# Fixed sets of PSUM banks for the MLP panels, layer norm features a tile sooner, and gates with 16 stationary columns

## The reference

```python
def sqrelu_mlp(x, w_up, w_down):
    return jnp.square(jax.nn.relu(x @ w_up)) @ w_down

for layer in range(2):
    if layer == 0:
        mix = ... @ w_out_even
    else:
        h = x @ w_in_odd                 # 1024 x 3088: q, k, v, and fl, one gate for each of 16 heads
        qf, kf, vf, fl = _split(h, ODD_SPLITS)
        mix = forgetting_attention(qf, kf, vf, fl, fox_f_bias) @ w_out_odd
    x = layer_norm(ALPHA * x + mix, gain[layer, 0], bias[layer, 0])
    x = layer_norm(ALPHA * x + sqrelu_mlp(x, w_up, w_down), gain[layer, 1], bias[layer, 1])
```

## Time and profile before

| | |
|---|---|
| median of three executions | 2456.62 us |
| profiled execution, its own time | 2456.84 us |
| its span in the profile | 2455.5 us |
| mean TensorE clock granted, of full speed | 0.959 |
| PE busy | 2286.5 us, 93% |
| DVE busy | 1043.5 us, 42% |
| ACT busy | 703.8 us, 29% |

### The profile page before, as it was taken

The page is one execution under the profiler, slowest core; times in us unless marked ns, Lnnn a source line. Parts: engine busy times, 40 slices in busy tenths (PEclk is TensorE's granted clock), DMA queues, the critical chain, the costliest instruction groups (busy, mean ns, idle before and its releaser), DMA issues.

```text
span 2455.5 us, 28478 instructions
## 1 busy us (share of the span) xinstructions
PE 2286.5 (93%) x11871; PEld 1686.7 (69%) x11871; DVE 1043.5 (42%) x1904; ACT 703.8 (29%) x1188; POOL 95.4 (4%) x96
## 2 busy tenths in 40 slices
PE   7998899979989999899788989999999999899998
PEld 6866687864434343587555778888787777788887
DVE  5347465342322233434566534233521455342335
ACT  4324354310100010223345223133223362231331
POOL 2001001010000000000000000000000000000000
PEclk9989899989999999999889999999989999999999
DMA  5232242359999999522100222323132201223230
GB/s 194 86 127 82 78 163 105 102 223 392 427 426 427 426 428 427 203 81 69 69 1 1 90 100 103 103 86 103 36 132 86 86 2 39 100 102 103 86 103 34
DMA packets 106740, 370.34 MB, mean 151 GB/s; under 512 B 15040, under 2 KB 20672, under 8 KB 94320
## 3 DMA queue, kind: packets, MB, share of 16 engines
q1 hardware_dynamic: 103584, 361.65, 39.1%
q0 software_dynamic: 3024, 6.83, 0.9%
HBM read 368.38 MB, written 4.19 MB: 152 GB/s over the span
## 4 chain that ended last, share of the span: by engine, by line
PE 78%; DMA 10%; DVE 8%; ACT 2%; issue 1%; POOL 1%; SPq 0%; DVEq 0%; ACTq 0%; POOLq 0%
PE PB L450 52%; PE PB L1898 8%; PE PB L467 5%; PE PB L460 4%; PE PB L769 4%; DMA Z<-in_w_exp_gate 4%; PE PB L661 3%; DMA FL_raw<-in_w_exp_gate 1%; DMA FH_raw<-in_w_exp_gate 1%; DMA Z<-in_w_exp_down 1%; PE PB L785 1%; DVE W L442 1%; DMA FL_raw<-in_w_exp_down 1%; PE PB L666 1%; ACT W L434 1%
## 5 line engine op out<-in xcount | busy, mean ns | idle before, releaser
L442 DVE TENSOR_TENSOR W<-R,W 128x2048 fp32r<-128x2048 f32 (+1 forms) x128 | 291.4, 2277 | 663.1 <-ACT W L434 663.0
L450 PE MATMUL PB<-W,FH 128*128 128x512 f32 (+1 forms) x1792 | 558.4, 394 | 8.1 <-DVE FL L823 6.7
L434 ACT ACTIVATE W<-R 128x2048 fp32r<-128x2048 f32 (+1 forms) x128 | 243.5, 1903 | 678.8 <-PE PB L450 671.7
L450 PEld LDWEIGHTS PB<-W,FH 128*128 128x128 f32 x1792 | 332.4, 190 | 77.4 <-DVE FL L823 8.1
L450 PE MATMUL PB<-W,hid 128*128 128x512 f32 x1536 | 349.6, 389 | 1.0 <-DVE X L2923 1.0
L450 PE MATMUL PB<-W,FL 128*128 128x512 f32 (+1 forms) x896 | 348.8, 389 | 0.0
L450 PE MATMUL PB<-FH,W 128*128 128x512 f32 (+1 forms) x1152 | 327.4, 369 | 15.6 <-ACT nsp L2878 14.3
L450 PEld LDWEIGHTS PB<-W,hid 128*128 128x128 f32 x1536 | 288.1, 188 | 61.0 <-DVE X L2923 1.4
L450 PEld LDWEIGHTS PB<-FH,W 128*128 128x128 f32 x1152 | 210.7, 191 | 52.1 <-ACT nsp L2878 14.7
L450 PE MATMUL PB<-FL,W 128*128 128x512 f32 (+1 forms) x576 | 212.2, 368 | 0.0
L450 PEld LDWEIGHTS PB<-W,FL 128*128 128x128 f32 x896 | 169.7, 189 | 35.4
(11 more groups left out here) (329 smaller groups left out, 2643.8 us busy)
## 6 DMA issues: line engine op xcount, KB each, us to landing
R<-in_mlp_w_up SPq DMA_DIRECT2D x32, 1024.0 KB, 5.3
R<-in_mlp_w_down SPq DMA_DIRECT2D x32, 1024.0 KB, 5.0
Z<-in_w_exp_down SPq DMA_DIRECT2D x14, 2048.0 KB, 30.6
Z<-in_w_exp_up SPq DMA_DIRECT2D x13, 2048.0 KB, 36.4
R<-in_w_exp_gate SPq DMA_DIRECT2D x11, 2048.0 KB, 32.3
W_raw<-in_w_exp_up SPq DMA_DIRECT2D x10, 2048.0 KB, 31.3
R<-in_w_exp_up SPq DMA_DIRECT2D x9, 2048.0 KB, 30.9
R<-in_w_in SPq DMA_DIRECT2D x12, 1024.0 KB, 5.4
```

The source lines that it names most:

```text
L434: k.A.e.activation(w.splits[w.split_of[u]][0][:, 0:m], w.rows(u), ACT.Copy).then_inc(*w.hi.tick(u))
L442: k.V.e.tensor_tensor(wl[:, 0:m], w.rows(u), wh[:, 0:m].bitcast(F32), ALU.subtract).then_inc(*w.lo.tick(u))
L450: ins = te.matmul(bank, l, r, start=(start and n == 0), stop=(stop and n == len(terms) - 1), skip_group_check=True)
```

## The change

**Banks.** The first up panel still takes four banks of PANELS. These four are now set 0 of the layer, and the other four banks are set 1. Up panel j takes set j mod 2, and down half h takes set h. The last down half of layer 0 takes the two banks of set 1 that are not in FLIPS, and the first two of set 0. In both layers set 0 comes out as banks 4, 5, 0, 1 and set 1 as 2, 3, 6, 7.

**Features.** DVE makes the low part of tile 0's features after centring tile 1 (before: tile 2), and that of tile 1 after centring tile 2 (before: behind tile 2's scale and a cut of weights). ACT makes the high parts of both ahead of a cut that stood between them. PE turns tile 0 one step of 12 products earlier.

**Gates.** ACT and DVE cut the 16 gate columns into `forget_hi` and `forget_lo` (128 x 128 each). PE takes them as the stationary operand, 16 columns wide, and moves the 512 tokens of FH and FL: 24 products into the first 16 partitions of a bank. DVE copies that out (16 x 512), PE turns it in four turns behind the second step of the next panel, into a bank of FLIPS, and the logarithms go on from there.

```diff
+    def numbers(self, keys):
+        return tuple(self.banks.index(self.where[key]) for key in keys)
...
+        self.forget_w = [nc.alloc_sbuf_tensor_at(name, [P, KT, 16], FR, offset=self.z_at + 4 * at)
+                         for name, at in (("forget_hi", 16128), ("forget_lo", 16256))]
... act_out_ln
     act_features(k, ("ln", n), 0)
+    act_features(k, ("ln", n), 1)
     act_cut(k, u0 + 4)
-    act_features(k, ("ln", n), 1)
... dve_out_ln, and with other units dve_mlp
         dve_ln_center(k, n, i)
-        if i == 2:
-            dve_features(k, ("ln", n), 0)
+        if i in (1, 2):
+            dve_features(k, ("ln", n), i - 1)
         if i == 3:
             dve_cut(k, u0 + 5)
         dve_ln_scale(k, n, i)
         if i == 2:
             dve_cut(k, u0 + 4)
-            dve_features(k, ("ln", n), 1)
... pe_ln_behind
-    return {5: lambda: pe_ln(k, n, 0), 6: lambda: pe_ln(k, n, 1)}
+    return {4: lambda: pe_ln(k, n, 0), 6: lambda: pe_ln(k, n, 1)}
... pe_mlp
-            banks = [k.banks.take(T, ("up", layer, c, j, f), k.relued.at(layer, c, j, f),
-                                  of=Banks.PANELS if first else Banks.ALL) for f in range(4)]
+            keys = [("up", layer, c, j, f) for f in range(4)]
+            banks = [k.banks.take(T, key, k.relued.at(*key[1:]), of=Banks.PANELS if first else fours[j % 2]) for key in keys]
+            if first:
+                fours = [k.banks.numbers(keys)]
+                fours.append(tuple(b for b in Banks.ALL if b not in fours[0]))
...
-            of = Banks.PANELS if (c, half) == (1, 1) else Banks.ALL
+            of = fours[half]
+            if (c, half) == (1, 1) and layer == 0:
+                of = tuple(b for b in fours[1] if b not in Banks.FLIPS) + fours[0][0:2]
...
-                if (layer, c, half) == (0, 1, 1) and (q, i) in ((3, 2), (2, 3)):
+                if (layer, c, half) == (0, 1, 1) and (q, i) in ((2, 2), (2, 3)):
                     pe_ln(k, 1, i - 2)
... pe_odd
+    def turn_gates():
+        bank = k.banks.take(T, ("flog",), k.dve_step.at("forget", "logits"), of=Banks.FLIPS)
+        T.wait_ge(*k.dve_step.at("forget", "copied"))
+        flips(k, bank, [k.o_gates[:, 128 * i:128 * i + 128] for i in range(NT)]).then_inc(*k.pe_step.tick("forget"))
...
-                   behind=({} if p else {1: lambda: pe_ln(k, 1, 2), 2: lambda: pe_ln(k, 1, 3)}))
+                   behind={0: {1: lambda: pe_ln(k, 1, 2), 2: lambda: pe_ln(k, 1, 3)}, 1: {1: turn_gates}}.get(p, {}))
         if p == 0:
-            bank = k.banks.take(T, ("flog",), k.dve_step.at("forget", "logits"))
-            T.wait_ge(*k.c6_in.at(3))
-            for i in range(NT):
-                at = slice(128 * i, 128 * i + 128)
-                ins = group(te, bank[:, 16 * i:16 * i + 16],
-                            [(F[:, c, at].bitcast(F32), k.o_wf[:, c, :]) for F in (k.FH, k.FL) for c in range(KT)])
-            ins.then_inc(*k.pe_step.tick("forget"))
+            bank = k.banks.take(T, ("gates",), k.dve_step.at("forget", "copied"))
+            T.wait_ge(*k.dve_step.at("forget", "parts"))
+            terms, (wh, wl) = [], k.forget_w
+            for c in range(KT):
+                terms += three((wh[:, c, :], wl[:, c, :]), (k.FH[:, c, :], k.FL[:, c, :]))
+            products(te, bank[0:16, :], terms, True, True).then_inc(*k.pe_step.tick("gates by head"))
... act_odd, first panel
+            A.wait_ge(*k.c6_in.at(3))
+            ae.activation(k.forget_w[0][:], k.o_wf, ACT.Copy).then_inc(*k.act_step.tick("forget", "high"))
... dve_odd, first panel
+            V.wait_ge(*k.act_step.at("forget", "high"))
+            ve.tensor_tensor(k.forget_w[1][:], k.o_wf, k.forget_w[0][:].bitcast(F32), ALU.subtract).then_inc(
+                *k.dve_step.tick("forget", "parts"))
... dve_forget
+    V.wait_ge(*k.pe_step.at("gates by head"))
+    ve.tensor_copy(k.o_gates, k.banks["gates",][0:16, :]).then_inc(*k.dve_step.tick("forget", "copied"))
```

More of the change, by code:

```diff
@@ L2883, in act_mlp @@
         for n in range(8):
-            if layer == 0 and c and n >= 6:
-                act_features(k, ("ln", 1), n - 6)
+            if layer == 0 and c and n == 6:
+                act_features(k, ("ln", 1), 0)
+                act_features(k, ("ln", 1), 1)
             if u0 + 10 + n < end:
@@ L2929, in dve_mlp @@
                 if (c, half) == (1, 1):
-                    if layer == 0 and i == 2:
-                        dve_features(k, ("ln", 1), 0)
+                    if layer == 0 and i in (1, 2):
+                        dve_features(k, ("ln", 1), i - 1)
                     if layer == 0 and i == 3:
@@ L2936, in dve_mlp @@
                         dve_cut(k, u0 + 16)
-                        dve_features(k, ("ln", 1), 1)
             if (c, half) != (1, 1):
@@ L2961, in odd_views @@
     k.o_lf, k.o_fb = Z[:, 12416:12480], Z[:, 12480:12496]
+    k.o_gates = k.tmp[0][0:16, 512:1024]
     k.o_lw = Z[:, 15616:16128].rearrange("p (i m) -> p i m", i=4)
@@ L3043, in act_odd @@
         act_cut(k, u0 + 2 * p + 2)
+        if p == 0:
+            A.wait_ge(*k.c6_in.at(3))
+            ae.activation(k.forget_w[0][:], k.o_wf, ACT.Copy).then_inc(*k.act_step.tick("forget", "high"))
         for i in range(NT):
@@ L3114, in dve_forget @@
     l3 = lf.rearrange("p (i h) -> p i h", i=4)
+    V.wait_ge(*k.pe_step.at("gates by head"))
+    ve.tensor_copy(k.o_gates, k.banks["gates",][0:16, :]).then_inc(*k.dve_step.tick("forget", "copied"))
     V.wait_ge(*k.c6_in.at(3))
     V.wait_ge(*k.pe_step.at("forget"))
-    ve.tensor_tensor(l3, k.banks["flog",][:, 0:64].rearrange("p (i h) -> p i h", i=4),
+    ve.tensor_tensor(l3, k.banks["flog",][:].rearrange("p (i m) -> p i m", i=4)[:, :, 0:16],
                      k.o_fb.unsqueeze(1).to_broadcast([P, 4, 16]), ALU.add).then_inc(*k.dve_step.tick("forget", "logits"))
```

## The result

| | before | after |
|---|---|---|
| median | 2455.95 us (4 runs, 2454.28 to 2457.24) | 2418.64 us (4 runs, 2418.55 to 2421.92) |
| ratio, 95% interval | | 0.9849 [0.9833, 0.9865] |
| profiled execution | 2456.84 us, span 2455.5 | 2421.92 us, span 2420.3 |
| mean granted clock | 0.959 | 0.963 |

The changed kernel is 37.3 us faster by the medians. The forecast was 2419.4 us, 0.8 us from the median. That nearness is partly luck, and the part on why the prediction was right says where. The profiled execution of the changed kernel is the slowest of the four, so the two profiles differ by only 35.2 us.

What follows compares the result with a forecast made beforehand. PE, busy 93% of the span, was taken as the bound. Banks 20.4 + gates 19.3 + features 0.5 - clock 3.0 = 37.2 us off 2456.84 gave 2419.6; the median, 0.2 lower, 2419.4 us (8 in 10: 2414 to 2428).

Steps and rivals of the forecast that it cites:

- Banks, 20.4 us: MLP panels of both layers: relu waits 14.3 us, half clock behind them 5.1 and a last-down-half wait 1.0 go.
- both slow starts: Products behind the two relu waits in the MLPs: 2.3 + 2.8 = 5.1 us lost at half clock would go.
- Gates, 19.3 us: Odd layer's head: 16.6 us from cheaper gates, 1.5 from products behind at full clock, 1.2 from the running sums' wait.
- Features, starting times: Panels after three norms: 0.7 and 0.5 us sooner at the projections, 0.7 later at the MLP's; 0.5 gained.
- Features, the clock: Idle gaps ahead of the next panel at three norms: two clock falls, 3.0 us lost (bounds 0 and 4.5).
- the earlier fall: Even layer's norm before the change, clock 0.50 behind 3.04 us idle: gives nothing back beyond the starting times.
- Gates at half clock: Rival: the new gate products run at half clock, adding 6.9 us, 2426.3 us; chance 0.15.
- The stall stays: Rival: PE's wait in the MLP is for weights, not banks, and remains; 19.4 us, 2438.8 us; chance 0.04.
- Slower: Rival: odd layer's clock falls in the gates and following panels stay slow; two panels give 2469.9 us; chance 0.01.
- The clock holds at all gaps: Rival: no clock fall behind the idle gaps at the three norms, 3.0 us less, 2416.4 us; chance 0.14.

Runs made afterwards that it cites:

- the filled kernel: The changed kernel with three plain float32 products of 512 columns, result unread, in PE's gap at each of three norms: 2413.13 us, ratio 0.9829.
- the gates four times over: The changed kernel with each of the 24 products of the odd layer's gates issued four times, same sum: 2432.72 us in one execution.
- the cut first: The changed kernel with VectorE cutting the next panel's first unit of weights ahead of tile 2's scale: 2415.77 us, ratio 0.9831.

## Why the prediction was right

**Banks, 20.4 us: right in each term.** The part alone gave 20.6. Nothing took the wait's place, and both slow starts went with it. The experiment with the relus first confirms the mechanism that the prediction read from ACT's queue: with the relus ahead of one cut on ACT and DVE, 11.5 of the 14.3 us went.

**Gates, 19.3 us: right.** 19.4 in its stretch. The 24 products took 5.6 us (0.232 each), so the lower end of the range of 5.4 to 10.9 us was nearly right, and the four turns 0.35 us instead of 0.5. The running sums lost their wait, and the 60 products behind took 13.63 us as forecast.

**Features, starting times: right.** The prediction said 0.7 and 0.5 us sooner at the two projections' norms and 0.7 later at the MLP's. From mark to first product the changed kernel was 0.56 and 0.37 us sooner; at the MLP's norm the turns of tile 3 were done 0.59 us later. PE stood idle for 3.16, 2.7 and 3.16 us where 3.3, 3.1 and 3.3 were forecast, and for 0.85 us ahead of tile 0's turn where 1.1 were. In all the starts gave 0.3 us where 0.5 were forecast.

**Features, the clock: the right count, too small a price.** This is the one term of the sum that was mis-sized. Two falls at 1.5 us each were forecast, 3.0 in all. There were two falls, at the two norms of projections. From the first product to the turns of tile 3 the changed kernel lost 2.6 us at the even layer's norm and 1.4 at the odd's, 4.0 in all. The fall at the odd layer's norm cost what was forecast, 1.4 against 1.5. The one at the even layer's norm cost more because it lasted longer: PE worked at 0.50 for some 5.7 us there and for some 3.3 us at the other. So the price of a fall was sized rightly but for this one. With the features part alone the same measure gives 1.4 us at the even layer's norm (1407.98 to 1419.88, where before it took 10.53 us) and 1.5 at the odd layer's, with 1.6 at the MLP's. The prediction had one fall to go by, and took its price for both; why one of them lasted longer stays open. Filling the gaps gave back 2.5 + 1.4 us, which confirms the size. Also right is that the earlier fall, before the change, gave nothing back: it had cost next to nothing, since the panel started 16.9 us behind the mark with it (even layer) and 16.7 without it (odd layer).

**The sum.** 20.6 + 19.4 - 3.7 = 36.3, against 36.0 in the tail and 37.2 forecast. The forecast of the time started from the median of three executions, 2456.62 us; a fourth took that median to 2455.95. So the median came out 0.8 us below the forecast and not above it by luck: it rests on that and on the untouched first 1390 us, in which the profiled executions of these kernels differ by several us (first mark at 1388.8 to 1396.7).

**The rivals.** Gates at half clock: refuted, also over 22 us of them. The stall stays: refuted by the banks alone. Slower: nothing of it is seen. (Its count of 1.7 panels left out the 6.9 us that the same rival puts on the gates; with them (37.2 - 6.9) / 21.8 = 1.4 panels would have decided the sign.) The clock holds at all gaps: it is what the filled kernel shows, at 4.0 us less, but not what the changed kernel did.

**Open.** Why a gap lets the clock fall in one execution and not in the other. The wait of 2.68 us at the MLP's norm left the clock at 1.00 in both profiles of the changed kernel and lowered it in two others, with the features part alone and with the gates four times over. The wait of 2.34 us with the cut first lowered it, too. Nor why a fall behind the same gap has two lengths. At the even layer's norm it cost 2.6 us in both profiles of the changed kernel, 1.4 with the features part alone, and 1.3 less than the 2.6 with the gates four times over, where the added work comes some 370 us later. The length of the gap alone doesn't decide it here, and I tried nothing that separates the length from what PE did before.

## What to carry to other kernels

When a wait is shortened upstream of a resource that doesn't move (here the cut of weights), look for where the idle time goes: gathered in one piece ahead of the next panel it costs the idle time plus a slow start, here 1.4 to 2.6 us where the clock fell. If such a gap can't be closed, a few products that nobody reads can keep TensorE's clock up at no cost, as long as they end before the wait does; three products did so here, and two in a shorter gap. And to judge parts worth 1 to 4 us, measure between marks that all the kernels share; the medians of whole executions didn't separate them.

## What the runs showed of the hardware

- A product of 512 moving columns costs nearly the same with 16 stationary columns as with 128: 0.232 us from one start to the next (24 of them, and 72 further ones) against 0.227, at clock 1.00. The old form, 128 stationary columns and 16 moving, kept PE as busy, and the clock was at 0.50 from about 5 us on the earlier trace rows.
- Behind gaps of 2.7 to 3.2 us ahead of a panel the clock fell in all but two of the cases looked at (the 2.7 us of the changed kernel, in both its profiles). A fall cost 1.3 to 1.6 us, and 2.6 at one norm. Three plain float32 products of 512 columns in the gap kept it at 1.00.
- The same waiting time isn't the same price: 2.68 us cost nothing in two profiles and 1.6 us in two others. A shorter one, 2.34 us, lowered the clock as well.
- A stretch that no edit touched, the old gates and the 60 products behind them, took 37.7 us in two kernels (before, banks alone) and 40.9 in two others (features alone, relus first). In the latter the clock fell about 2.5 us into the gates instead of 5; what brings that about isn't shown.
